# Order of the first products and of the first norm's loads in a hybrid encoder kernel

## The chip, the cores and the metric

One NeuronCore of one Trainium2 chip runs the whole program. The metric is the device time of one execution in microseconds (us). TensorE (PE) does the matrix products, VectorE (DVE) and ScalarE (ACT) the elementwise work, SyncE (SP) issues nearly all transfers; ACT issues two of them before the change.

## The reference, cut to what matters

Two layers of a trunk over 256 tokens of 1,024 values. The change touches only the first norm and the query columns of the first layer's projection:

```
h = layer_norm(x, ln_in_g, ln_in_b)
for i in range(2):
    z = h @ w_in[i]                     # columns: q 1024 | k 256 | v 256 | xr 1024 | yr | ga | gr
    attn = local_attention(rope(q), rope(k), v)
    rnn  = bidirectional_rg_lru(xr) * gelu(yr)
    h = layer_norm(a*h + (sig(ga)*(attn@w_pa) + sig(gr)*(rnn@w_pr)) @ w_out)
    h = layer_norm(a*h + ffn(h) + ple(h, p[i]))
```

Everything is float32. The kernel gets that precision from float32r products: each operand is cut into a high part (a rounded copy) and a low part (what the rounding left), and three products are summed: high x high, high x low, low x high.

## The kernel before

Tokens stand in two tiles of 128 (t = 0, 1); `c` numbers the two halves of 512 features. Weights come as items of 1 MB (128 x 2048 values). The first items are q0 part 0 (item 0), q0 part 1 (item 1), q1 part 0 (item 2), q1 part 1 (item 3), xr0 half 0 (item 4), xr0 half 1 (item 5), xr1 half 0 (item 6), the first gate block (item 7). A part of a query unit holds 512 columns for one half of the 1,024 input rows. An item is loaded into `raw`; ACT casts it to the high part (`split_hi`, L822), and DVE subtracts to get the low part (`split_lo`, L1128), which is written over `raw`. Items 0 to 3 take homes 0 to 3, item 4 takes home 4 and item 5 home 0 again, so the load of item 5 waits until TensorE is done with item 0 (`load_item`, L440: it waits for the count `s_products` that the last product on the former item gives, here `("q0", "half")`); item 6 waits in the same way for item 1, and so on.

The activations take this way: DVE takes statistics and normalises tile t (`add_ffn`, `norm_rest`: L1145 to L1175, the last four instructions are L1171 and L1174 for c = 0 and for c = 1), TensorE turns each half with four transposes into a bank (`turn_h`, L662, L654), ACT writes the high part x_hi (`x_parts`, L832), DVE the low part x_lo (`x_parts`, L1190).

Each engine runs its own list in order, written out by hand. In the first layer before the change:

- SP: rows of tile 0 (x0), item 0, the norm's gain and offset rows copied to all partitions (`load_norm`, one transfer of 1 MB), items 1 and 2, small parameters, items 3 and 4, then the waiting loads of items 5, 6 and so on.
- ACT: waits for x0, issues the rows of tile 1 (x1) and the rope table, casts item 0, x_hi of tile 0, casts items 1 and 2, x_hi of tile 1, casts items 3 and 4, empties the banks of q0, casts item 5, takes one exponential (L1019), casts item 6.
- DVE: norm of tile 0, low part of item 0, x_lo of tile 0, low part of item 1, norm of tile 1, x_lo of tile 1, low parts of items 2 to 4, `params` (L1200; it stops at L1211 for ACT's exponential), low parts of items 5, 6.
- TensorE (`token_part`, L525, twelve products of 512 columns each, four k-steps of three): q0 part 0 and part 1 for tile 0; turns of tile 1; then the other six parts, so 24 products, the turns, 72 products. Each waits until both parts of its item are there (`weights`, L519, waits for `s_split`). Behind them come the xr units with products of 256 columns.

Of the kernel before, what the change touches and what calls it, by code (L numbers as in the profile page):

```python
# [34 lines left out]
P = 128  # L35
DEPTH, SEQ, D = 2, 256, 1024
# [7 lines left out]
TT = SEQ // P  # L44
# [109 lines left out]
def in_pe_order(l):  # L154

    steps = [("q0", 0), ("q0", "half"), ("q0", 1), ("q1", "half"), ("q1", 0), ("q1", 1), ("xr0", 0), ("xr0", 1)]
    for i, name in enumerate(WITH_BLOCK):
        feature = UNITS[name][0] == "feature"
        steps += [(name, 0 if feature else "half")]
        steps += [(f"rg{i // RNN_BLOCKS}", (i % RNN_BLOCKS, g)) for g in range(2)]  # L160
        steps += [(name, 1)] if feature else [(name, 0), (name, 1)]
    steps += [(name, part) for name in ("pa0", "pa1", "pr0", "pr1") for part in ("half", 0, 1)]
    steps += [("wo0", 0), ("wo1", 0), ("wo0", "half"), ("wo1", "half"), ("wo0", 1), ("wo1", 1), ("pg0", 0)]
    steps += [("ple", (part, t)) for part in range(2) for t in range(TT)]
    steps += [("pg0", "half"), ("pg0", 1), ("pg1", "half"), ("pg1", 0), ("pg1", 1)]
    for j in range(FF_GROUPS):
        steps += [(f"{u}{j}", hh) for u in "gv" for hh in range(2)]
        if 0 < j < LAST:
            steps += [(f"d{j - 1}", part) for part in ("half", 0, 1)]
    return steps + [(f"d{LAST}", (0, 0)), (f"d{LAST}", (0, 1)), (f"d{LAST - 1}", "half"), (f"d{LAST - 1}", 1),  # L170
                    (f"d{LAST}", (1, 0)), (f"d{LAST}", "half"), (f"d{LAST}", (1, 1))]
# [31 lines left out]
RING = {}  # L203
# [44 lines left out]
def hybrid_encoder(nc, a, out):  # L248
    with ExitStack() as ctx:
# [131 lines left out]
        s_lnp = sem("lnp_loaded")  # L381
        s_small = sem("rnn_params_loaded")
# [41 lines left out]
        def _(sp):  # L424
# [38 lines left out]

            sp.dma_start(h[:, 0, :], a["x"][0, 0:P, :]).then_inc(s_h[0], 16)
            for l in range(DEPTH):
                head = ITEM[l, "q0", 0]
                load_item(head)
                load_norm(l, 0)
# [43 lines left out]
        def _(pe):  # L512
# [139 lines left out]

            def turn(dst, src):
                return nc.tensor.transpose(dst, src, ident[:])  # L654
# [64 lines left out]
            for l in range(DEPTH):  # L719
# [3 lines left out]
                if l == 0:  # L723
                    turn_h(l, 0, 0)
                x_ready(l, 1)
                token_part(l, "q0", 0, 0, x)
                x_ready(l, 2)
                token_part(l, "q0", 1, 0, x).then_inc(s_products, 1)
                turn_h(l, 0, 1, [0])
                if l:  # L730
                    token_part(l, "q1", 0, 0, x)
                turn_h(l, 0, 1, [1])
                x_ready(l, 3)
                token_part(l, "q0", 0, 1, x).then_inc(s_products, 1)
                x_ready(l, 4)
                token_part(l, "q0", 1, 1, x).then_inc(s_products, 1)
                if l == 0:
                    token_part(l, "q1", 0, 0, x)
                token_part(l, "q1", 0, 1, x).then_inc(s_products, 1)
                for t in range(TT):  # L740
                    token_part(l, "q1", 1, t, x).then_inc(s_products, 1)
# [75 lines left out]
        def _(act):  # L817
# [186 lines left out]
            act.wait_ge(s_h[0], 16)  # L1004
            act.dma_start(h[:, 1, :], a["x"][0, P:SEQ, :]).then_inc(s_h[1], 16)
            act.dma_start(rope[:], a["rope"]).then_inc(s_rope, 16)
            for l in range(DEPTH):
# [5 lines left out]
                x_parts(l, 2, [(1, 0), (1, 1)], 1.0)  # L1013
# [109 lines left out]
        def _(dve):  # L1123
# [23 lines left out]
            def norm_rest(l, n, t):  # L1147
# [20 lines left out]
                dve.wait_ge(s_lnp, 32 * l + 16 * n + 16)  # L1168
                for c in range(2):
                    at = slice(512 * c, 512 * c + 512)  # L1170
# [246 lines left out]
            for l in range(DEPTH):  # L1417
# [3 lines left out]
                if l == 0:  # L1421
                    split_to(l, "q0", 0, 0)
                    x_parts(l, 0, [(0, 0), (0, 1)], 1.0)
                    split_to(l, "q0", 1, 0)
# [175 lines left out]
```

## Time and profile before

| | us |
|---|---|
| median of 3 runs | 975.0 |
| lowest and highest run | 973.78 and 975.1 |
| the profiled execution | 974.05 |
| its span, first to last instruction | 972.2 |
| TensorE busy in it | 938.5 (97%) |
| VectorE busy | 727.5 (75%) |
| ScalarE busy | 576.1 (59%) |

1.85 us of the profiled execution lie around its span. Times in the trace count from the start of the span. Matmuls overlap, so their listed durations are longer than the distance between their starts; the sums below use the distance. In the first 16 us TensorE has only eight transposes to do; from there it is nearly always busy.

### The profile page before, as it was taken

The page shows a single profiled execution, that of the slowest core. Times are in us where ns is not written, and L with a number is a line of the kernel's source. Part 1 is how long each engine was busy: PE and PEld are TensorE (multiplying, and loading weights), DVE is VectorE, ACT ScalarE, POOL GpSimd, SP SyncE. Part 2 cuts the span into 40 slices and gives each one's busy share as a digit, 9 for nine tenths or more (in the row PEclk, how much of TensorE's full clock was granted, in tenths as well). Part 3 has the DMA queues.
Part 4 walks back from the last instruction along what each step waited for, and adds up shares of the span by engine and source line. Part 5 has one row for each costly group of instructions (what it writes and reads, how often), then busy time and mean ns, then how long its engine had stood idle before and what let it go on. Part 6 is the DMA issues. An engine that isn't in the chain of part 4 may idle for free.

```text
span 972.2 us, 12457 instructions
## 1 busy us (share of the span) xinstructions
PE 938.5 (97%) x5056; PEld 805.3 (83%) x5056; DVE 727.5 (75%) x974; ACT 576.1 (59%) x726; POOL 1.4 (0%) x9
## 2 busy tenths in 40 slices
PE   4999999999999999999999989999999999999996
PEld 3898888987788888888889879888877888888885
DVE  6778788796857876867867698888867686866755
ACT  3479789954256655546345889887434655645540
POOL 0000000000000000000000000000000000000000
PEclk9999999999999999999999999999999999999998
DMA  8455435675466556555454645455645955655621
GB/s 307 152 174 195 132 109 161 204 260 207 154 197 217 193 174 200 189 176 200 166 176 119 206 127 179 130 174 200 243 134 173 296 177 182 203 177 186 204 87 43
DMA packets 117752, 174.61 MB, mean 180 GB/s; under 512 B 3904, under 2 KB 78400, under 8 KB 117056
## 3 DMA queue, kind: packets, MB, share of 16 engines
q1 hardware_dynamic: 117408, 173.27, 53.7%
q8 instruction: 40, 0.66, 0.3%
q10 hardware_dynamic: 288, 0.56, 0.2%
q14 instruction: 16, 0.13, 0.0%
HBM read 172.76 MB, written 1.05 MB: 179 GB/s over the span
## 4 chain that ended last, share of the span: by engine, by line
PE 91%; DVE 4%; DMA 2%; ACT 2%; issue 1%; SPq 0%; DVEq 0%
PE ring L564 19%; PE ring L515 15%; PE ring L517 15%; PE ring L516 15%; PE ring L566 9%; PE misc L515 4%; PE misc L516 4%; PE misc L517 4%; PE misc L654 2%; PE misc L692 1%; PE misc L712 1%; DMA sb_r_raw<-in_w_ple_gate_dram 1%; DMA sb_lnp<-in_ln_dram 1%; DVE sb_w_lo L1128 1%; DVE sb_tmp L1294 0%
## 5 line engine op out<-in xcount | busy, mean ns | idle before, releaser
L1128 DVE TENSOR_TENSOR sb_w_lo<-sb_raw,sb_w_hi 128x2048 fp32r<-128x2048 f32 (+1 forms) x140 | 299.2, 2151 | 65.1 <-ACT sb_w_hi L822 64.9
L822 ACT CAST sb_w_hi<-sb_raw 128x2048 fp32r<-128x2048 f32 (+1 forms) x140 | 249.9, 1798 | 19.4 <-DMA sb_raw<-in_w_in_dram 4.8
L564 PE MATMUL ring<-sb_x_both,sb_w_hi 128*128 128x512 f32 x544 | 193.1, 399 | 0.0
L566 PE MATMUL ring<-sb_x_both,sb_w_lo 128*128 128x256 f32 x544 | 152.8, 281 | 0.0
L515 PE MATMUL ring<-sb_w_hi,sb_x_both 128*128 128x512 f32 x304 | 122.7, 404 | 6.4 <-DVE sb_x_both L1194 6.4
L564 PEld LDWEIGHTS ring<-sb_x_both,sb_w_hi 128*128 128x128 f32 x544 | 102.2, 188 | 25.4
L516 PE MATMUL ring<-sb_w_lo,sb_x_both 128*128 128x512 f32 x304 | 120.1, 395 | 0.0
L517 PE MATMUL ring<-sb_w_hi,sb_x_both 128*128 128x512 f32 x304 | 120.0, 395 | 0.0
L566 PEld LDWEIGHTS ring<-sb_x_both,sb_w_lo 128*128 128x128 f32 x544 | 102.8, 189 | 0.3
L515 PEld LDWEIGHTS ring<-sb_w_hi,sb_x_both 128*128 128x128 f32 x304 | 58.2, 191 | 19.3 <-DVE sb_x_both L1194 7.9
L515 PE MATMUL ring<-sb_x_both,sb_w_hi 128*128 128x256 f32 x256 | 73.0, 285 | 0.0
L517 PE MATMUL ring<-sb_x_both,sb_w_lo 128*128 128x256 f32 x256 | 72.4, 283 | 0.0
L516 PE MATMUL ring<-sb_x_both,sb_w_hi 128*128 128x256 f32 x256 | 72.4, 283 | 0.0
L517 PEld LDWEIGHTS ring<-sb_w_hi,sb_x_both 128*128 128x128 f32 x304 | 58.1, 191 | 12.7
L516 PEld LDWEIGHTS ring<-sb_w_lo,sb_x_both 128*128 128x128 f32 x304 | 58.2, 192 | 11.4
L940 ACT COPY sb_soft<-ring 128x512 f32<-128x512 f32 x24 | 14.1, 588 | 87.4 <-PE ring L566 87.4
L515 PE MATMUL misc<-sb_w_hi,sb_a_hi 128*128 128x512 f32 x144 | 56.3, 391 | 0.0
L516 PE MATMUL misc<-sb_w_lo,sb_a_hi 128*128 128x512 f32 x144 | 56.1, 390 | 0.0
L517 PE MATMUL misc<-sb_w_hi,sb_a_lo 128*128 128x512 f32 x144 | 56.0, 389 | 0.0
L836 ACT ACTIVATE sb_x_both<-misc 128x512 fp32r<-128x512 f32 x24 | 13.9, 596 | 67.8 <-PE misc L654 67.8
L516 PEld LDWEIGHTS ring<-sb_x_both,sb_w_hi 128*128 128x128 f32 x256 | 49.1, 192 | 0.1
L515 PEld LDWEIGHTS ring<-sb_x_both,sb_w_hi 128*128 128x128 f32 x256 | 49.1, 192 | 0.1
(184 smaller groups left out, 1854.7 us busy)
## 6 DMA issues: line engine op xcount, KB each, us to landing
sb_raw<-in_w_in_dram SPq DMA_DIRECT2D x42, 1024.0 KB, 5.3
sb_raw<-in_w_up_dram SPq DMA_DIRECT2D x34, 1024.0 KB, 5.3
sb_raw<-in_w_down_dram SPq DMA_DIRECT2D x18, 1024.0 KB, 4.9
sb_raw<-in_w_proj_attn_dram SPq DMA_DIRECT2D x8, 1024.0 KB, 5.1
sb_raw<-in_w_proj_rnn_dram SPq DMA_DIRECT2D x8, 1024.0 KB, 5.1
sb_hb<-in_w_up_dram SPq DMA_DIRECT2D x8, 1024.0 KB, 5.2
sb_raw<-in_w_out_dram SPq DMA_DIRECT2D x6, 1024.0 KB, 5.6
sb_raw<-in_w_ple_gate_dram SPq DMA_DIRECT2D x6, 1024.0 KB, 5.5
```

The source lines that it names most:

```text
L515: nc.tensor.matmul(dst, lhs[0], rhs[0], start=first, stop=False)
L516: nc.tensor.matmul(dst, lhs[0], rhs[1], start=False, stop=False)
L517: return nc.tensor.matmul(dst, lhs[1], rhs[0], start=False, stop=last)
L564: nc.tensor.matmul(bank_of(*key), hi[:, cols], x_both[:, k], start=k == 0, stop=False)
L566: last = nc.tensor.matmul(bank_of(*key)[:, 0:SEQ], lo[:, cols], x_hi[:, k], start=False, stop=k == KT - 1)
L654: return nc.tensor.transpose(dst, src, ident[:])
L692: last = nc.tensor.matmul(misc[:, i // 2, SEQ * (i % 2):SEQ * (i % 2 + 1)], qkT[:, GROUP * g + i, b * P:(b + 1) * P], qkT[:, HEADS + g, :] ...
L712: last = nc.tensor.matmul(misc[:, 2, :], v[:, kb, r // TT, :], pT[:, kb, :, :], start=kb == 0, stop=kb == TT - 1)
L822: nc.scalar.copy(hi_at[home][:, 0:size], raw_at[home][:, 0:size]).then_inc(s_hi_part, 1)
L836: nc.scalar.activation(x_hi[:, 4 * c:4 * c + 4, t * P:(t + 1) * P], misc[:, 2 * t + c, :].rearrange("p (k t) -> p k t", k=4), ACT.Copy, sc ...
L940: nc.scalar.copy(half_of(name)[:, hh], ring[:, pair:pair + 2, SEQ:2 * SEQ]).then_inc(s_taken, 1)
L1128: nc.vector.tensor_tensor(lo_at[home][:, 0:size], raw_at[home][:, 0:size], hi_at[home][:, 0:size].bitcast(F32), ALU.subtract).then_inc(s_s ...
```

## The change

- SP now issues: x0; the left half (columns 0 to 511 of gain and offset, 0.5 MB) of the norm's rows with a semaphore of its own; item 0; the right half (0.5 MB); x1 (moved here from ACT); items 1 and 2; the rest as before.
- DVE waits for the left half only ahead of c = 0 of tile 0, for the right half ahead of all else. It no longer takes the low parts of items 0 and 1 between the norms; it goes from x_lo of tile 0 to the norm of tile 1, and takes items 0 to 4 after x_lo of tile 1.
- ACT waits for x1 instead of x0 ahead of the rope table's issue. Item 3 is cast between x_hi of (tile 1, c = 0) and x_hi of (tile 1, c = 1).
- TensorE in the first layer first does the passes with the high weight parts (`high_pass`: eight products, x_hi and x_lo with the high part): q0 part 0, q0 part 1, q1 part 0 for tile 0, turn of (1, 0), q1 part 1 for tile 0, turn of (1, 1), the four parts for tile 1; then the 32 products with the low weight parts (`low_pass`). The number of products is the same, 96. `("q0", "half")` now comes from the low pass.
- The second layer's list is the one of before, as a function.

```diff
-    steps = [("q0", 0), ("q0", "half"), ("q0", 1), ("q1", "half"), ...]
+    steps = [("q0", 0), ("q0", "half"), ("q0", 1)] if l else [("q0", "half"), ("q0", 0), ("q0", 1)]
...
+            def load_first_norm(c, signal):
+                at = slice(512 * c, 512 * c + 512)
+                sp.dma_start(lnp[:, :, at], a["ln"][0:1, :, at].to_broadcast((P, 2, 512))).then_inc(signal, 16)
...
             sp.dma_start(h[:, 0, :], a["x"][0, 0:P, :]).then_inc(s_h[0], 16)
+            load_first_norm(0, s_lnp_left)
             for l in range(DEPTH):
                 head = ITEM[l, "q0", 0]
                 load_item(head)
-                load_norm(l, 0)
+                if l == 0:
+                    load_first_norm(1, s_lnp)
+                    sp.dma_start(h[:, 1, :], a["x"][0, P:SEQ, :]).then_inc(s_h[1], 16)
+                else:
+                    load_norm(l, 0)
...
+            def high_pass(l, name, hh, t, ready):
+                n = ITEM[l, name, hh]
+                hi = hi_at[HOME[n]]
+                pe.wait_ge(s_hi_part, n + 1)
+                if hh == 0:
+                    pe.wait_ge(s_emptied[RING[l, name, t][0]], free(l, name, t))
+                pe.wait_ge(s_x_hi, value("x_hi", l, ready))
+                for i, x in enumerate((x_hi, x_lo)):
+                    if i:
+                        x_ready(l, ready)
+                    for k in range(4):
+                        nc.tensor.matmul(bank_of(l, name, t), x[:, 4 * hh + k, t * P:(t + 1) * P],
+                                         hi[:, 512 * k:512 * k + 512], start=hh == 0 and i == 0 and k == 0, stop=False)
...
+            def first_query_units(l):
+                turn_h(l, 0, 0)
+                high_pass(l, "q0", 0, 0, 1)
+                high_pass(l, "q0", 1, 0, 2)
+                high_pass(l, "q1", 0, 0, 1)
+                turn_h(l, 0, 1, [0])
+                high_pass(l, "q1", 1, 0, 2)
+                turn_h(l, 0, 1, [1])
+                for hh in range(2):
+                    for name in ("q0", "q1"):
+                        high_pass(l, name, hh, 1, 3 + hh)
+                for name in ("q0", "q1"):
+                    low_pass(l, name, 0, 0)
+                    low_pass(l, name, 0, 1).then_inc(s_products, 1)
+                    low_pass(l, name, 1, 0).then_inc(s_products, 1)
+                    low_pass(l, name, 1, 1).then_inc(s_products, 1)
...
-            act.wait_ge(s_h[0], 16)
-            act.dma_start(h[:, 1, :], a["x"][0, P:SEQ, :]).then_inc(s_h[1], 16)
+            act.wait_ge(s_h[1], 16)
             act.dma_start(rope[:], a["rope"]).then_inc(s_rope, 16)
...
-                x_parts(l, 2, [(1, 0), (1, 1)], 1.0)
+                x_parts(l, 2, [(1, 0)], 1.0)
+                if l == 0:
+                    split_to(l, "q1", 1, 0)
+                x_parts(l, 3, [(1, 1)], 1.0)
...
                 if l == 0:
-                    split_to(l, "q0", 0, 0)
                     x_parts(l, 0, [(0, 0), (0, 1)], 1.0)
-                    split_to(l, "q0", 1, 0)
                     add_ffn(l, 1, 0)
```

## Rows read from the trace of the kernel before

**Rows 1.** The page's part 4: the chain that ended last, by engine.

```profile
PE 91%; DVE 4%; DMA 2%; ACT 2%; issue 1%; SPq 0%; DVEq 0%
```

**Rows 2.** Waits of TensorE in the whole span: total us, times, longest us.

```profile
PE misc L654 <- DVE sb_h L1174: 13.7, 5, 12.0
PE ring L515 <- DVE sb_x_both L1194: 6.4, 4, 2.2
PE misc L654 <- DVE sb_qk L1245: 4.9, 2, 2.4
```

**Rows 3.** TensorE by time: start us, us, work, [idle <- who released it].

```profile
16.11 0.80 PE L515 MATMUL ring<-sb_w_hi,sb_x_both 128*128 128x512 f32 x1 [1.69 <-DVE sb_x_both L1194]
...
24.23 0.60 PE L654 MATMUL misc<-sb_ident,sb_h 128*128 128x128 f32 x4
...
26.24 0.50 PE L515 MATMUL ring<-sb_w_hi,sb_x_both 128*128 128x512 f32 x1 [0.29 <-DVE sb_x_both L1194]
26.57 0.39 PE L516 MATMUL ring<-sb_w_lo,sb_x_both 128*128 128x512 f32 x1
...
42.67 0.28 PE L515 MATMUL ring<-sb_x_both,sb_w_hi 128*128 128x256 f32 x1
```

**Rows 4.** VectorE in order of time, 7 to 42 us.

```profile
7.53 0.16 DVE L1166 SCALAR_TENSOR_TENSOR sb_mv<-sb_mv 128x1 f32<-128x1 f32 x1
10.27 0.75 DVE L1171 SCALAR_TENSOR_TENSOR sb_h<-sb_h,sb_mv,sb_lnp 128x512 f32<-128x512 f32 x1 [2.58 <-DMA sb_lnp<-in_ln_dram]
...
19.09 1.28 DVE L1145 BATCH_NORM_STATS2 sb_st<-sb_h 128x6 f32<-128x512 f32 x2
...
36.47 0.17 DVE L1213 TENSOR_SCALAR sb_lam_t<-sb_lam_t 128x16 f32<-128x16 f32 x1 [2.13 <-ACT sb_lam_t L1019]
...
39.36 4.48 DVE L1128 TENSOR_TENSOR sb_w_lo<-sb_raw,sb_w_hi 128x2048 fp32r<-128x2048 f32 x2
```

**Rows 5.** Transfers of the first 60 us: size, us from issue to landing.

```profile
sb_lnp<-in_ln_dram SPq DMA_DIRECT2D x1, 1024.0 KB, 8.6
sb_h<-in_x_dram SPq DMA_DIRECT2D x1, 512.0 KB, 3.7
sb_h<-in_x_dram ACTq DMA_DIRECT2D x1, 512.0 KB, 6.8
```

**Rows 6.** Stretch from 4 to 10 us: the last number is GB/s moved.

```profile
4.00:10.00 6.00, 0.00 (x0) 0.00 (x0) 2.97 (x13) 3.18 (x2) 0.00 (x0) 1.00 1.03 417
```

**Rows 7.** ScalarE in order of time, 5 to 37 us.

```profile
5.32 1.28 ACT L822 ACT_TABLE_LOAD   x1 [5.32 <-DMA sb_h<-in_x_dram]
7.13 1.90 ACT L822 CAST sb_w_hi<-sb_raw 128x2048 fp32r<-128x2048 f32 x1 [0.52 <-DMA sb_raw<-in_w_in_dram]
...
14.96 3.69 ACT L822 CAST sb_w_hi<-sb_raw 128x2048 fp32r<-128x2048 f32 x2
24.86 0.60 ACT L836 ACTIVATE sb_x_both<-misc 128x512 fp32r<-128x512 f32 x1 [6.21 <-PE misc L654]
...
34.42 1.91 ACT L822 CAST sb_w_hi<-sb_raw 128x2048 fp32r<-128x2048 f32 x1 [1.83 <-DMA sb_raw<-in_w_in_dram]
```

**Rows 8.** SP's queue, 20 to 37 us: the issues of items 5 and 6.

```profile
29.26 3.09 SPq L454 DMA_DIRECT2D sb_raw<-in_w_in_dram  x2
```

**Rows 9.** The same sixteen transposes in layer 1 and layer 2.

```profile
93.28 3.57 PE L654 MATMUL misc<-sb_ident,sb_qk 128*128 128x128 f32 x16 [2.42 <-DVE sb_qk L1245]
...
565.39 1.97 PE L654 MATMUL misc<-sb_ident,sb_qk 128*128 128x128 f32 x16 [2.43 <-DVE sb_qk L1245]
```

**Rows 10.** Stretches around three stalls; granted clock is third from the end.

```profile
93.30:96.70 3.40, 3.40 (x17) 3.40 (x18) 3.40 (x3) 3.37 (x8) 0.00 (x0) 0.51 0.74 239
...
240.00:250.00 10.00, 7.82 (x35) 6.13 (x34) 7.50 (x7) 5.55 (x5) 0.00 (x0) 1.00 0.33 122
710.00:720.00 10.00, 7.76 (x28) 5.89 (x27) 6.68 (x6) 5.62 (x5) 0.00 (x0) 0.83 0.40 147
```

**Rows 11.** Waits of ScalarE from 42 to 75 us.

```profile
ACT sb_xT L843 <- PE ring L517: 8.8, 4, 4.2
```

More of the change, by code:

```diff
@@ L154, in in_pe_order @@
 def in_pe_order(l):
-    steps = [("q0", 0), ("q0", "half"), ("q0", 1), ("q1", "half"), ("q1", 0), ("q1", 1), ("xr0", 0), ("xr0", 1)]
+    steps = [("q0", 0), ("q0", "half"), ("q0", 1)] if l else [("q0", "half"), ("q0", 0), ("q0", 1)]
+    steps += [("q1", "half"), ("q1", 0), ("q1", 1), ("xr0", 0), ("xr0", 1)]
     for i, name in enumerate(WITH_BLOCK):
@@ L381, in hybrid_encoder @@
         s_lnp = sem("lnp_loaded")
+        s_lnp_left = sem("first_lnp_left_loaded")
         s_small = sem("rnn_params_loaded")
@@ new lines, in low_pass @@
+            def low_pass(l, name, hh, t):
+                hi, lo = weights(l, name, hh)
+                for k in range(4):
+                    last = nc.tensor.matmul(bank_of(l, name, t), x_hi[:, 4 * hh + k, t * P:(t + 1) * P],
+                                            lo[:, 512 * k:512 * k + 512], start=False, stop=hh == 1 and k == 3)
+                return last
+            def first_query_units(l):
[14 more added lines that the diff above has]
+                    low_pass(l, name, 1, 1).then_inc(s_products, 1)
@@ new lines, in query_units @@
+            def query_units(l):
+                x = (x_hi, x_lo)
+                x_ready(l, 1)
+                token_part(l, "q0", 0, 0, x)
+                x_ready(l, 2)
+                token_part(l, "q0", 1, 0, x).then_inc(s_products, 1)
+                turn_h(l, 0, 1, [0])
+                token_part(l, "q1", 0, 0, x)
+                turn_h(l, 0, 1, [1])
+                x_ready(l, 3)
+                token_part(l, "q0", 0, 1, x).then_inc(s_products, 1)
+                x_ready(l, 4)
+                token_part(l, "q0", 1, 1, x).then_inc(s_products, 1)
+                token_part(l, "q1", 0, 1, x).then_inc(s_products, 1)
+                for t in range(TT):
+                    token_part(l, "q1", 1, t, x).then_inc(s_products, 1)
@@ L723, in _ @@
                 if l == 0:
[L724 to L741, printed above, removed]
+                    first_query_units(l)
+                else:
+                    query_units(l)
                 feature_unit(l, "xr0")
@@ L1167, in norm_rest @@
                                                    op1=ALU.mult).then_inc(s_ln_step, 1)
-                dve.wait_ge(s_lnp, 32 * l + 16 * n + 16)
                 for c in range(2):
+                    if (l, n, t, c) == (0, 0, 0, 0):
+                        dve.wait_ge(s_lnp_left, 16)
+                    else:
+                        dve.wait_ge(s_lnp, 32 * l + 16 * n + 16)
                     at = slice(512 * c, 512 * c + 512)
```

## The prediction

> **What bounds the kernel now.** I read the chain that ended last first: TensorE holds 91% of it [rows 1], so the time can move only by when TensorE starts, by how long it is idle, and by its clock. Its list of waits has three entries [rows 2]: 12.0 us before the first transposes, four stalls for x_lo and two for the rotated queries, the longest of each 2.2 and 2.4 us. The products start at 16.11 us and the query units end at 42.67 us, where the first product of 256 columns starts [rows 3]. The change touches only what lies before. From there to the rotated queries TensorE has no wait [rows 2], so I ask when the query units end afterwards and whether an item is late behind them.
>
> What sets the start at 16.11? VectorE has its small norm steps done at 7.69 us (7.53 + 0.16) and then waits 2.58 us for the gain rows until 10.27 [rows 4]. ScalarE has the high part of item 0 long done (7.13 + 1.90 = 9.03 [rows 7]). So the left half, loaded early, attacks a real wait, and the high-first order a second one: a low part costs VectorE 2.2 us (4.48 for two [rows 4]), and one sits ahead of x_lo, which released the first product [rows 3].
>
> **Landing times after.** From 4 to 10 us the core takes in 417 GB/s [rows 6]. x0 landed at 4.43 (issued at 0.74, 3.7 us [rows 5]). I take what stands behind it on SP's queue to land in order at that rate. Test on before: item 0 would land at 4.43 + 1.05/0.417 = 6.95; ScalarE's wait for it ended at 7.13 [rows 7]. After: left half (0.52 MB) 5.7, item 0 8.2, right half 9.5, x1 10.7, and 10.8 with the slightly lower rate at the end. x1 now stands behind 2.1 MB; bounds for it are 10.0 and 11.2, the latter where it landed from ScalarE's own queue (4.43 + 6.8 [rows 5]).
>
> **The new wait on ScalarE.** It used to wait for x0; now for x1, and its queue runs in order: behind the wait stand the rope issue, the table load, the cast of item 0, x_hi. Before, the table load began 0.89 us after x0 (5.32 against 4.43 [rows 7]). So: 10.8 + 0.89 = 11.7, load 1.28, cast from 13.0, the next instruction 1.8 us later (two casts back to back take 3.69 [rows 7]), x_hi of (0, 0) from 14.8 to 15.4 (0.60 [rows 7]), first product at **15.45**. The tile's other steps are ready sooner: c = 0 is normalised at 7.7 + 1.5 = 9.2, c = 1 at 9.5 + 1.5 = 11.0, transposed by 12.2. Of the roughly 4 us that the two edits free, ScalarE's wait takes all but 0.66 us (16.11 - 15.45).
>
> **The first 24 products.** From 16.11 to the transposes at 24.23 they take 8.12 us [rows 3], which fits twelve at 0.43 and twelve at 0.23 us, so half of them run at half speed. Afterwards they are 24 as well, with an idle gap ahead of them again; I take 8.12 and keep 1 us either way for when the clock rises. Their high parts are there: items 1 and 2 are cast by 17.7 and 19.5 (15.9 + 3.69), wanted near 18.9 and 21.7; VectorE's norm of tile 1 starts at 16.7 where it started at 19.09 [rows 4], so h is early. The transposes of (1, 0) start at 15.45 + 8.12 = 23.57.
>
> **The cast of item 3.** TensorE's next pass, q1 part 1, waits for item 3's high part, and ScalarE casts it only behind x_hi of (1, 0), which waits for just these transposes. Before, x_hi began 0.63 us after the transposes did (24.86 against 24.23 [rows 3, 7]) and the next product started at 26.24, 2.01 us after them, the second turn included. After: 0.63, then the cast 0.49 behind x_hi, 1.90 long: 3.02 us, of which TensorE is idle 2.5. So 23.57 + 3.02 = 26.6; eight products 1.9 (0.33 for the first, then 0.227 each: 71 of them fill 26.57 to 42.67 [rows 3]); the second turn 0.45, now on its own (four transposes are listed at 0.60 us, which is the upper bound, with the next work overlapping them [rows 3]; the lower is half of that, 0.45 the middle); 64 products 14.5. The query units end at **43.47**, against 42.67: **+0.8 us**. In the low passes no low part is late: VectorE starts them at 30.5 and needs 2.2 each, wanted from 36.2, 38.0, 39.8 and 41.7. The extra SP issues lie under transfers that take 1.3 us and more; the rope table, now later, is wanted past 90 us.
>
> **The load of item 5.** It waits for the last product on item 0. It used to be issued at 29.26 [rows 8]; now item 0 is in use until its low pass: 28.95 + 40 x 0.227 = 38.0, issued at 38.2. It took 5.16 us to land (34.42 [rows 7]), with ample time left. After: landed 43.4, cast, the exponential at 43.4 + 1.8 = 45.2 right behind it; VectorE stands in `params` for that and resumes 0.24 us later (36.47 against 34.42 + 1.81 [rows 4, 7]): 45.4. From there to its next low part 2.89 us (36.47 to 39.36 [rows 4]): 48.3, plus 2.28 is **50.6**. TensorE wants item 5 when xr0's first half is done: 43.47 + 5.76 (48 products, 0.12 apart) = 49.2. A new stall of **1.4 us**.
>
> **Behind it.** Item 6 and the later ones have a unit of 5.8 us each to arrive. ScalarE is some 1.6 us later against TensorE when it empties the first xr bank, but it waited 8.8 us for such banks from 42 to 75 us [rows 11], so I take the lag as regained and the shift as handed on one for one.
>
> **The clock.** A stall of about 2.4 us can bring it down. The same sixteen transposes took 3.57 us behind a stall of 2.42 and 1.97 behind one of 2.43 [rows 9]; the granted clock behind the first was 0.51 (1.2 GHz) for 3.4 us [rows 10]. Of two stalls for x_lo, one left it at 1.00 (2.4 GHz), the other at 0.83 over ten us [rows 10]. Two in four, 1.6 us a time: bounds 0 and 1.6 for the new stall; I take the middle, **+0.8**, since rows of equal length lie at both ends. The Trainium skill (TensorE: Matmul & The Clock Gate, HAM oscillation) warns only of longer idle gaps; by that the term would be 0 and the time 0.8 less. The 0.51 row speaks against it.
>
> **Sum.** -0.66 (start) + 1.01 (3.02 instead of 2.01) + 0.45 (second turn) + 1.4 (item 5) + 0.8 (clock) = +3.0 us. The profiled execution took 974.05, so 977.05 by it; it lies 0.95 under the median of 975.0, which is what is compared. Forecast: 975.0 + 3.0 = **978.0**.
>
> **Rivals.**
> - *Item 5 is not late.* If its transfer or `params` is 1.4 us quicker than taken, 0.8 for the query units and 0.8 for the clock remain: 976.6; with the clock up 975.8. For it: the stall is a difference of two long sums. Against it: all its terms are rows.
> - *The lag adds up.* If ScalarE's 1.6 us isn't regained before the rotated queries, where VectorE already releases TensorE [rows 2], it comes on top: 979.6. Against it the 8.8 us of slack [rows 11].
> - *ScalarE isn't held* (the other side). If the table load and the first cast run as soon as item 0 lands at 8.2, or x1 lands far sooner, the first product waits only for the turn of c = 1 and starts at 12.1, 3.35 us sooner: 978.0 - 3.35 = 974.65, not slower; with the clock up or item 5 in time as well, under 973.05. It decides by when the cast of item 0 starts: each us before 13.0 is one of the end. Against it: before, nothing of ScalarE's list went ahead of x0 [rows 7]. The Trainium skill (ScalarE: Activation LUTs, Step-by-step: what each stage is for) has the table load placed right before the activation that needs it; by that it can't slip ahead, and the trace agrees with its 5.32.
> - *The change doesn't do what it says.* If the first pass waited for low parts after all, it would start past 18 us and end past 980. The diff shows no such wait.
>
> **How the numbers follow.** A measurement of this kernel can tell about 0.2% (1.95 us): faster is under 973.05, slower over 976.95. Forecast 0.52 (977.2 to 978.8 without and with the fall of the clock, nine in ten of it over the bound); item 5 in time 0.20 (nearly all within 0.2%); lag adds up 0.10 (slower); not held 0.14 (0.09 within, 0.05 faster); the last one 0.04 (slower). Slower 0.47 + 0.10 + 0.04 = 0.61, within 0.05 + 0.20 + 0.09 = 0.34, faster 0.05. The range takes the forecast, the first two rivals, the bounds of x1's landing (0.8 below, 0.4 above) and some of the 1 us of the clock's rise: 975.3 to 980.3. Outside lie most of "not held" and the last rival.
>
> **What would show it.** In the changed kernel: VectorE's first L1171 at about 7.7 us with no wait, ScalarE's table load near 11.7 (at 5 to 9 the forecast falls), first product near 15.45; a wait of TensorE of about 2.5 us for ScalarE's `sb_w_hi` near 24 to 26.6; first 256-column product near 43.5; a wait of about 1.4 us for VectorE's `sb_w_lo` near 49.2; the wait for rotated queries still 2.4 us. If the first product is at 12 and the two waits are small, the change gains and I am wrong in the start.

## The result, and the profile of the changed kernel

| | before | changed |
|---|---|---|
| median of 9 runs each, us | 974.0 (973.2 to 977.4) | 980.0 (977.1 to 981.3) |
| profiled execution, us | 974.05, span 972.2 | 980.0, span 978.2 |
| first product starts, us | 16.11 | 16.37 |
| first product of 256 columns (end of the query units), us | 42.67 | 45.96 |
| transposes of the rotated queries, us | 93.28 | 98.70 |

The ratio is 1.005, 95% interval 1.0037 to 1.0062: the change makes the kernel 4.9 us slower (3.6 to 6.0). The ratio is over all runs; the two medians alone are 6.0 apart. The forecast was +3.0 us. The sign is right and the 980.0 lies inside the range; the size was taken too small by about 2 us.

Runs of one kernel lie in steps of 1.5 to 2 us, and the mean granted clock goes down with each step (before: 0.996 at 971.9 us, 0.994 near 973.7, 0.992 near 975.2, 0.991 near 977.3). One fall of the clock costs about as much, 1.6 us (measured below), so a single profile can be off its kernel's median by one fall or more.

The waits of TensorE come first. A line is engine and line that wait, for whom, us in total, how often, the longest:

```profile
PE misc L725 <- DVE sb_h L1235: 12.4, 4, 9.4
PE misc L725 <- DVE sb_qk L1306: 4.9, 2, 2.4
PE ring L677 <- ACT sb_x_both L892: 2.8, 1, 2.8
PE ring L677 <- ACT sb_w_hi L878: 2.5, 1, 2.5
PE ring L527 <- DVE sb_w_lo L1186: 1.9, 1, 1.9
```

The three entries of before [rows 2] have become six; the one left out here is the wait for x_lo behind line 527, 4.6 us in two, which stood there before as well. Two entries are the forecast's: 2.5 us for ScalarE's `sb_w_hi` (item 3) and 1.9 us for VectorE's `sb_w_lo` (item 5). The 2.8 us for ScalarE's x_hi are the hold of ScalarE. What the changed kernel no longer has are the 1.69 us for x_lo ahead of the first product and the 0.29 us at tile 1 [rows 3].

TensorE's timeline up to item 5 (start, us, engine, line, what, count, idle time ahead and its releaser):

```profile
16.37 8.13 PE L677 MATMUL ring<-sb_w_hi,sb_x_both 128*128 128x512 f32 x24 [2.81 <-ACT sb_x_both L892]
24.34 0.60 PE L725 MATMUL misc<-sb_ident,sb_h 128*128 128x128 f32 x4
27.41 3.03 PE L677 MATMUL ring<-sb_w_hi,sb_x_both 128*128 128x512 f32 x8 [2.47 <-ACT sb_w_hi L878]
38.70 7.42 PE L684 MATMUL ring<-sb_w_lo,sb_x_both 128*128 128x512 f32 x32
45.96 0.28 PE L527 MATMUL ring<-sb_x_both,sb_w_hi 128*128 128x256 f32 x1
53.74 0.39 PE L527 MATMUL ring<-sb_x_both,sb_w_hi 128*128 128x256 f32 x1 [1.87 <-DVE sb_w_lo L1186]
```

The first product starts at 16.37, hardly moved. The transposes of (1, 0) start at 24.34, the next product only at 27.41. Eight products then take 3.03 us: the clock has fallen. At 53.74 the stall for item 5 ends.

What held the start, VectorE above and ScalarE below:

```profile
7.71 0.75 DVE L1232 SCALAR_TENSOR_TENSOR sb_h<-sb_h,sb_mv,sb_lnp 128x512 f32<-128x512 f32 x1
10.85 0.75 DVE L1232 SCALAR_TENSOR_TENSOR sb_h<-sb_h,sb_mv,sb_lnp 128x512 f32<-128x512 f32 x1 [1.60 <-DMA sb_lnp<-in_ln_dram]
12.12 0.38 ACTq L1061 DMA_DIRECT2D sb_rope<-in_rope_dram  x1
12.53 1.28 ACT L878 ACT_TABLE_LOAD   x1 [12.53 <-DMA sb_h<-in_x_dram]
13.83 1.90 ACT L878 CAST sb_w_hi<-sb_raw 128x2048 fp32r<-128x2048 f32 x1
```

VectorE normalises c = 0 at 7.71 with no wait, 2.56 us sooner than before [rows 4]: the left half does what it says. ScalarE takes none of that up. It waits for x1, issues the rope table at 12.12, loads its table, and casts item 0 only from 13.83, when tile 0 is already normalised (11.63 + 0.75 = 12.38) and transposed (12.44 + 1.12 = 13.56). The Trainium skill (TensorE: Matmul & The Clock Gate, Architectural detail: the array is 16× 32×32, not 1× 128×128) has ScalarE's and VectorE's queues as strictly first in, first out; the trace agrees, with everything of ScalarE's behind the wait.

Granted clock and transfer rate by stretch (busy time and instructions of each engine, then the clock as a share of full speed, the DMA engines' share, GB/s):

```profile
core 0: us, PE busy (x) PEld busy (x) DVE busy (x) ACT busy (x) POOL busy (x), PEclk, DMA share, GB/s
4.00:6.00 2.00, 0.00 (x0) 0.00 (x0) 1.41 (x4) 0.00 (x0) 0.00 (x0) 1.00 0.71 259
6.00:8.00 2.00, 0.00 (x0) 0.00 (x0) 1.76 (x11) 0.00 (x0) 0.00 (x0) 1.00 1.01 380
9.00:11.00 2.00, 1.09 (x4) 0.72 (x4) 0.40 (x2) 0.00 (x0) 0.00 (x0) 1.00 1.05 415
4.00:10.00 6.00, 0.60 (x3) 0.64 (x4) 4.38 (x15) 0.00 (x0) 0.00 (x0) 1.00 0.93 351
28.80:32.20 3.40, 3.40 (x12) 2.72 (x12) 0.24 (x1) 0.87 (x2) 0.00 (x0) 0.57 0.00 0
```

The core takes in 351 GB/s from 4 to 10 us where it took 417 [rows 6], and most of the shortfall lies in the first two us. The clock of 0.57 over the 3.4 us from 28.8 is half speed (1.2 GHz) for most of them.

The load of item 5, from SP's issue over ScalarE's cast and exponential to VectorE's low parts:

```profile
40.71 2.18 SPq L456 DMA_DIRECT2D sb_raw<-in_w_in_dram  x2
46.46 1.91 ACT L878 CAST sb_w_hi<-sb_raw 128x2048 fp32r<-128x2048 f32 x1 [3.33 <-DMA sb_raw<-in_w_in_dram]
48.51 0.17 DVE L1274 TENSOR_SCALAR sb_lam_t<-sb_lam_t 128x16 f32<-128x16 f32 x1 [4.43 <-ACT sb_lam_t L1077]
51.40 5.62 DVE L1186 TENSOR_TENSOR sb_w_lo<-sb_raw,sb_w_hi 128x2048 fp32r<-128x2048 f32 x3
```

It is issued at 40.71 where it was 29.26 [rows 8]; the cast waits for it until 46.46, the exponential until 48.27, VectorE waits 4.43 us for that and takes the low part only from 51.40, 2.34 us before TensorE gets it.

Far behind, the rotated queries' transposes and two stretches with a lower clock:

```profile
98.70 1.63 PE L725 MATMUL misc<-sb_ident,sb_qk 128*128 128x128 f32 x12 [2.42 <-DVE sb_qk L1306]
100.00:110.00 10.00, 10.00 (x44) 8.45 (x42) 8.46 (x13) 7.45 (x13) 0.00 (x0) 0.83 0.21 59
250.00:260.00 10.00, 10.00 (x39) 8.05 (x38) 8.00 (x17) 1.18 (x2) 0.00 (x0) 0.83 0.00 0
```

TensorE waits 2.42 us for the rotated queries, as before [rows 9]; they start 5.42 us later than at 93.28. So the shift of the first 54 us is handed on one for one. The span grew by 6.0. From 93 us on each profile has two falls of the clock with TensorE at work, at different places (before near 93 and at 710 to 720 [rows 10], the changed one at 100 and at 250); where the remaining 0.6 us comes from isn't shown.

The sum by these rows, against the forecast's terms:

| term | forecast | traces |
|---|---|---|
| start of the products | -0.66 | 16.37 - 16.11 = +0.26 |
| first 24 products | 0 | (24.34 - 16.37) - 8.12 = -0.15 |
| item 3's cast | +1.01 | 27.41 - 24.34 - 2.01 = +1.06 |
| second turn and the clock | +0.45 + 0.8 | (45.96 - 27.41) - (42.67 - 26.24) = +2.12 |
| item 5 | +1.4 | +1.87 |
| sum | +3.0 | +5.2 |

The fourth row can be parted by the run called filled below, in which the clock didn't fall: the second turn is +0.51 (16.94 - 16.43), the clock +1.61 (18.55 - 16.94).

### The profile page after: what moved, and what is told of

The parts are those of the page before. It is cut to its first block, busy times and chain, and to the rows that moved or that the text cites. A ratio compares the mean times of both kernels' runs of the same rounds, so it can differ in the third digit from the quotient of the medians.

```text
span 978.2 us, 12460 instructions
## 1 busy us (share of the span) xinstructions
PE 940.1 (96%) x5056; PEld 806.2 (82%) x5056; DVE 727.0 (74%) x974; ACT 575.7 (59%) x726; POOL 1.4 (0%) x9
## 4 chain that ended last, share of the span: by engine, by line
PE 89%; DVE 4%; DMA 3%; ACT 2%; issue 1%; SPq 0%; ACTq 0%; DVEq 0%
PE ring L576 18%; PE ring L527 14%; PE ring L528 14%; PE ring L529 14%; PE ring L578 9%; PE misc L527 4%; PE misc L529 4%; PE misc L528 4%; PE misc L725 2%; PE ring L677 2%; PE misc L763 1%; PE misc L783 1%; DMA sb_r_raw<-in_w_ple_gate_dram 1%; ACT sb_w_hi L878 1%; DMA sb_h<-in_x_dram 1%
## 5 line engine op out<-in xcount | busy, mean ns | idle before, releaser
L527 PE MATMUL ring<-sb_w_hi,sb_x_both 128*128 128x512 f32 x272 | 109.5, 403 | 4.6 <-DVE sb_x_both L1255 4.6
L528 PE MATMUL ring<-sb_w_lo,sb_x_both 128*128 128x512 f32 x272 | 107.2, 394 | 0.0
L529 PE MATMUL ring<-sb_w_hi,sb_x_both 128*128 128x512 f32 x272 | 107.0, 393 | 0.0
L527 PEld LDWEIGHTS ring<-sb_w_hi,sb_x_both 128*128 128x128 f32 x272 | 51.9, 191 | 15.7 <-DVE sb_x_both L1255 5.4
L529 PEld LDWEIGHTS ring<-sb_w_hi,sb_x_both 128*128 128x128 f32 x272 | 51.8, 190 | 11.3
L528 PEld LDWEIGHTS ring<-sb_w_lo,sb_x_both 128*128 128x128 f32 x272 | 51.8, 191 | 10.1
```

The source lines that it names most:

```text
L527: nc.tensor.matmul(dst, lhs[0], rhs[0], start=first, stop=False)
L528: nc.tensor.matmul(dst, lhs[0], rhs[1], start=False, stop=False)
L529: return nc.tensor.matmul(dst, lhs[1], rhs[0], start=False, stop=last)
```

## The experiments

Each was measured beside the kernel before on the same chip, 11 or 12 runs each, halves_swapped 6; before's own median was 973.9 to 975.0. The differences (95% interval) are the ratio to before, less one, times 974. "256" is the start of the first product of 256 columns, "qk" that of the rotated queries' transposes, both from the profile.

| kernel | median, us | against before, us | 256 | qk |
|---|---|---|---|---|
| before | | | 42.67 | 93.28 |
| changed | 980.0 | +4.9 (3.6 to 6.0) | 45.96 | 98.70 |
| order_only | 975.0 | +0.3 (-1.2 to 1.8) | 42.77 | 94.91 |
| loads_only | 976.5 | +2.0 (0.2 to 3.8) | 45.37 | 95.99 |
| act_free | 976.3 | +1.8 (0.6 to 2.9) | 41.56 | 93.61 |
| cast3_early | 975.2 | -0.5 (-1.8 to 0.9) | 40.76 | 92.78 |
| exp_early | 977.0 | +2.8 (1.4 to 4.4) | 45.73 | 96.34 |
| filled | 977.4 | +2.0 (0.3 to 3.9) | 44.00 | 96.64 |
| left_behind | 979.9 | +4.4 (2.8 to 5.8) | 45.18 | 97.39 |
| halves_swapped | 978.5 | +4.9 (3.1 to 6.7) | 45.34 | 97.54 |
| all_three | 971.3 | -3.0 (-4.8 to -1.3) | 39.94 | 90.55 |
| order_mended | 972.4 | -2.0 (-3.3 to -0.8) | 40.01 | 90.62 |
| item3_sooner | 972.4 | -2.4 (-3.7 to -1.2) | 39.35 | 89.97 |
| loads_free | 973.8 | +0.9 (-0.6 to 2.2) | 43.9 | 94.49 |

The columns 256 and qk are the sharper measure of a place, but they hold luck too: TensorE's first 24 products, the same work in all kernels, take 6.9 to 8.4 us from profile to profile. They start 0.43 us apart and end 0.23 apart, and what differs is when the one becomes the other (the clock column reads 1.00 throughout, so that this shows in the distances alone).

**The order alone** (the changed kernel with before's loads, x1 on ScalarE's queue):

```diff
             sp.dma_start(h[:, 0, :], a["x"][0, 0:P, :]).then_inc(s_h[0], 16)
-            load_first_norm(0, s_lnp_left)
...
-                if l == 0:
-                    load_first_norm(1, s_lnp)
-                    sp.dma_start(h[:, 1, :], a["x"][0, P:SEQ, :]).then_inc(s_h[1], 16)
-                else:
-                    load_norm(l, 0)
+                load_norm(l, 0)
...
-            act.wait_ge(s_h[1], 16)
+            act.wait_ge(s_h[0], 16)
+            act.dma_start(h[:, 1, :], a["x"][0, P:SEQ, :]).then_inc(s_h[1], 16)
...
```

> The changed kernel with the loads of before: one transfer for the norm's rows behind item 0, tile 1's rows from ScalarE's queue, ScalarE waiting for tile 0's rows only. Theory: first product behind the second turn near 14.5 (x_hi was at 13.07 before), the stall at item 3's cast of 2.5 us and that before xr0's second half of 1.2 to 1.9 us stay; 0.5 to 1.5 us slower than before, plus the clock's fall in some runs. Rival (the high-first order by itself gains): faster than before by 1 us or more.

```profile
13.90 7.48 PE L672 MATMUL ring<-sb_w_hi,sb_x_both 128*128 128x512 f32 x24
24.29 3.68 PE L672 MATMUL ring<-sb_w_hi,sb_x_both 128*128 128x512 f32 x8 [2.47 <-ACT sb_w_hi L873]
49.96 0.39 PE L522 MATMUL ring<-sb_x_both,sb_w_hi 128*128 128x256 f32 x1 [1.28 <-DVE sb_w_lo L1182]
```

The products start 2.2 us sooner than before, since none of them waits for a low part. All of it is given back: item 3's stall of 2.47 us with the clock's fall behind it (eight products in 3.68 us) brings the end of the query units to 42.77, where it was, and item 5 costs 1.28. The high-first order by itself is worth nothing here, as its casts and loads stand.

**The loads alone** (before, with the halves, x1 on SP and ScalarE's wait for it; order of products, casts and low parts as before), its wait alone:

```diff
...
-            act.wait_ge(s_h[0], 16)
-            act.dma_start(h[:, 1, :], a["x"][0, P:SEQ, :]).then_inc(s_h[1], 16)
+            act.wait_ge(s_h[1], 16)
...
```

> The kernel before with the load edits alone: halves of the first norm's rows, tile 1's rows on SP's queue, ScalarE waiting for them; the products in the old order. Theory: ScalarE is held to 12.1, cast of item 0 to 15.7, then its low part and x_lo on VectorE: first product near 18.6 instead of 16.1, no stalls at item 3 and item 5; 2.5 us slower than before, about 976.5. Rival (the loads help and the order of the products costs everything): first product at 14 or sooner and faster than before.

```profile
12.38 1.28 ACT L833 ACT_TABLE_LOAD   x1 [12.38 <-DMA sb_h<-in_x_dram]
18.55 0.80 PE L526 MATMUL ring<-sb_w_hi,sb_x_both 128*128 128x512 f32 x1 [5.17 <-DVE sb_x_both L1207]
```

The table load begins at 12.38 where it was 5.32 [rows 7], and the first product 2.44 us later than before. The halves are there, yet the loads as a whole cost 2.0 us by the ratio and 2.7 at both places of the profile.

**ScalarE not held** (the changed kernel, with ScalarE waiting for x0 ahead of the rope table; nothing else):

```diff
-            act.wait_ge(s_h[1], 16)
+            act.wait_ge(s_h[0], 16)
             act.dma_start(rope[:], a["rope"]).then_inc(s_rope, 16)
```

> The changed kernel with one edit: ScalarE waits for the rows of tile 0, not of tile 1, ahead of the rope table's issue. Theory (ScalarE is held by tile 1's rows): table load near 5.4, cast of item 0 near 9 to 11, first product right behind the second turn near 13.6 instead of 16.37, the other waits as they are; 2.8 us less than the changed kernel, about 976 to 977. Rival (the start is bound by the transfers or by VectorE, and the wait is hidden): first product stays near 16, time within 0.5 us of the changed kernel.

```profile
5.24 1.28 ACT L878 ACT_TABLE_LOAD   x1 [5.24 <-DMA sb_h<-in_x_dram]
9.44 1.90 ACT L878 CAST sb_w_hi<-sb_raw 128x2048 fp32r<-128x2048 f32 x1 [2.91 <-DMA sb_raw<-in_w_in_dram]
13.27 5.70 PE L677 MATMUL ring<-sb_w_hi,sb_x_both 128*128 128x512 f32 x16
24.62 2.13 PE L677 MATMUL ring<-sb_w_hi,sb_x_both 128*128 128x512 f32 x8 [2.47 <-ACT sb_w_hi L878]
```

One constant moves the first product from 16.37 to 13.27, 3.10 us. That is the price of the hold, and the ratios say the same (+1.8 instead of +4.9). Item 3's stall stays at 2.47 us, here without a fall of the clock. Behind the earlier start a wait of 0.63 us for item 2's cast is new, and the wait for item 5's low part is 1.2 us.

**Item 3's cast ahead of x_hi of (1, 0):**

```diff
-                x_parts(l, 2, [(1, 0)], 1.0)
                 if l == 0:
                     split_to(l, "q1", 1, 0)
+                x_parts(l, 2, [(1, 0)], 1.0)
                 x_parts(l, 3, [(1, 1)], 1.0)
```

> The changed kernel with one edit: ScalarE casts item 3 ahead of x_hi of (1, 0), not behind it. Theory (the cast order makes TensorE's stall at 25 to 27 us and with it the fall of the clock): that stall of 2.47 us is gone or under 0.5, the clock stays up there, the slower group of runs gets rarer; 2.5 us less without the clock, up to 4 us with it, about 976 to 977. Rival (item 3's transfer or VectorE's norm of tile 1 is next): a stall of over 1.5 us stays at the same place with another releaser.

```profile
16.25 7.40 PE L677 MATMUL ring<-sb_w_hi,sb_x_both 128*128 128x512 f32 x24 [2.81 <-ACT sb_x_both L892]
23.49 0.60 PE L725 MATMUL misc<-sb_ident,sb_h 128*128 128x128 f32 x4
23.84 2.10 PE L677 MATMUL ring<-sb_w_hi,sb_x_both 128*128 128x512 f32 x8
```

The stall is gone: product follows transposes after 0.35 us. No other wait comes in its place. At qk this kernel is 5.92 us ahead of the changed one, and the rows give each piece: start 0.12, first 24 products 0.73 (7.24 instead of 7.97; the clock rose sooner), transposes to product 2.72 (0.35 instead of 3.07), from there to the products of 256 columns 1.63 (16.92 instead of 18.55), item 5 0.71. Item 3's wait and the fall behind it are the largest single cost: 5.4 us by the ratios, 4.35 us (2.72 + 1.63) by the rows that belong to them. Without them the kernel can't be told from before.

**The exponential ahead of item 5's cast:**

```diff
-                split_to(l, "q1", 0)
-
+                if l:
+                    split_to(l, "q1", 0)
                 act.wait_ge(s_param_step, value("param_step", l, 1))
                 nc.scalar.activation(lam_t[:, 1], lam_t[:, 0], ACT.Exp).then_inc(s_param_exp, 1)
+                if l == 0:
+                    split_to(l, "q1", 0)
```

> The changed kernel with one edit: ScalarE takes the exponential that VectorE's parameter steps wait for ahead of the cast of item 5. Theory (item 5 is late because its cast, the exponential, the parameter steps and its low part stand in one chain): the stall of 1.87 us before xr0's second half is gone, VectorE takes the low part at once behind the cast, 1.9 us less than the changed kernel. Rival (the landing of item 5 alone makes it late): the stall stays over 1 us.

```profile
43.61 0.22 ACT L1077 ACTIVATE sb_lam_t<-sb_lam_t 128x16 f32<-128x16 f32 x1 [0.71 <-DVE sb_lam_t L1268]
45.68 1.90 ACT L878 CAST sb_w_hi<-sb_raw 128x2048 fp32r<-128x2048 f32 x1 [1.85 <-DMA sb_raw<-in_w_in_dram]
47.62 2.29 DVE L1188 TENSOR_TENSOR sb_w_lo<-sb_raw,sb_w_hi 128x2048 fp32r<-128x2048 f32 x1 [0.77 <-ACT sb_w_hi L878]
```

VectorE does its parameter steps while item 5 is still under way and waits only 0.77 us for the cast. TensorE has no wait for a low part any more; qk is 2.36 us sooner than in the changed kernel, of which 0.23 was there at 256 already; the ratios say 2.1. So the late load is not the cost by itself: the cost is that `params` stood between its cast and its low part.

**The stall of item 3 filled** with twenty transposes of the identity, whose result nobody reads (extra work; the result of the kernel is as before):

```diff
                 turn_h(l, 0, 1, [0])
+                for _ in range(20):
+                    turn(misc[:, 3, 0:P], ident[:])
                 high_pass(l, "q1", 1, 0, 2)
```

> The changed kernel with 20 transposes of the identity into an unused place, put where TensorE stands idle for item 3's cast; the computation is otherwise whole. Theory (the idle stretch brings the clock down in some runs): the stall's length stays (products resume near 27.4), the granted clock stays 1.00 from 27 to 32 us in the profile, and the upper group of runs (980 and over) vanishes, median near 977.5. Rival (the clock falls by something else, such as the phase of the earlier start): the clock falls behind it all the same and the upper group stays at about half of the runs.

```profile
27.06 2.12 PE L677 MATMUL ring<-sb_w_hi,sb_x_both 128*128 128x512 f32 x8 [0.30 <-ACT sb_w_hi L880]
27.00:32.00 5.00, 4.94 (x24) 4.08 (x25) 1.71 (x2) 2.35 (x3) 0.00 (x0) 1.00 0.00 0
```

TensorE waits as long as it did (the next product starts at 27.06, 0.35 sooner than in the changed kernel, since its first 24 products took less), but is idle for only 0.30 us of it. The clock stays at 1.00, eight products take 2.12 us, and from 27.06 to 44.00 pass 16.94 us instead of 18.55: **1.61 us is the price of the fall.** The ratios say 2.9, but their intervals (3.6 to 6.0 and 0.3 to 3.9) allow 1.6 as well. Of the six profiles with this stall unfilled (changed, order_only, exp_early, left_behind, halves_swapped, act_free), five show the fall; since one doesn't, filled's profile alone would be weak evidence, and its runs have to speak as well. The upper group didn't vanish but nearly did, as expected: one of 12 runs is at 980 us or over, where the changed kernel has five of 9, and the median of its runs' mean clocks is 0.994 instead of 0.992.

**Which half is slow.** Two kernels ask why x1 landed late: the left half behind item 0, and the two halves swapped (the right one first).

```diff
-            load_first_norm(0, s_lnp_left)
...
                 if l == 0:
+                    load_first_norm(0, s_lnp_left)
                     load_first_norm(1, s_lnp)
```

> The changed kernel with the left half of the norm's rows issued behind item 0, ahead of the right half. In the changed kernel the rate fell to 215 GB/s from 4 to 5 us, and tile 1's rows landed 1.3 us later than worked out. Theory (the small strided transfer right behind the first one leaves the engines short): from 4 to 7 us the rate is over 380 again, tile 1's rows land near 11.0, and with them table load, cast and first product come 0.9 us sooner, near 15.5; about 1 us less than the changed kernel. Rival (the halves cost the same wherever they stand): the landing stays near 12 and the first product near 16.3.

```profile
4.00:6.00 2.00, 0.00 (x0) 0.00 (x0) 1.72 (x7) 0.00 (x0) 0.00 (x0) 1.00 1.05 399
6.00:8.00 2.00, 0.00 (x0) 0.00 (x0) 1.25 (x7) 0.00 (x0) 0.00 (x0) 1.00 0.94 257
```

```diff
-            load_first_norm(0, s_lnp_left)
+            load_first_norm(1, s_lnp_left)
...
-                    load_first_norm(1, s_lnp)
+                    load_first_norm(0, s_lnp)
...
-                    if (l, n, t, c) == (0, 0, 0, 0):
+                    if (l, n, t, c) == (0, 0, 0, 1):
```

> The changed kernel with the right half of the norm's rows loaded at the first place and the left one behind item 0; VectorE needs the left one first, so its c = 0 waits for it. Theory (a half is slow by its place as the first transfer of these rows, not by which columns it holds): the rate from 4 to 6 us is again under 320 GB/s, and tile 1's rows land near 12 as in the changed kernel; the first product stays near 16.3 since ScalarE sets it. Rival (the left columns themselves are slow): the rate falls behind item 0, from 7 to 9 us, instead.

```profile
4.00:6.00 2.00, 0.00 (x0) 0.00 (x0) 1.29 (x2) 0.00 (x0) 0.00 (x0) 1.00 0.90 250
```

The slow stretch moves with the first half (257 GB/s from 6 to 8 us when it goes behind item 0) and does not care which columns it holds (250 from 4 to 6 us with the right one first). The second half runs at the common rate (415 GB/s from 9 to 11 us in the changed kernel, while it lands). Neither kernel differs from the changed one in time by more than the intervals: with ScalarE held, x_hi waits for ScalarE, and it is of no use that VectorE is early. I had put left_behind's rate over 380 until 7 us and its first product at 15.5; the slow stretch only moved, x1 was late all the same (ScalarE released at 11.77), and the product came at 16.01.

**All three edits together** (ScalarE free, item 3's cast and the exponential early):

> The changed kernel with the three edits together: ScalarE waits for tile 0's rows only, casts item 3 ahead of x_hi of (1, 0), takes the exponential ahead of the cast of item 5. Theory (the three waits are what eats the gain, and they add up): first product near 13.3, none of the three stalls over 0.7 us, first 256-column product near 39.5 instead of 42.67, about 3 us less than the kernel before: 971.5. Rival (the transfers are next: items 1 to 3 land too late for the earlier products): a stall of 1 us or more for a high part whose cast waited for its transfer, and less than 2 us of gain.

```profile
21.06 1.90 ACT L878 CAST sb_w_hi<-sb_raw 128x2048 fp32r<-128x2048 f32 x1 [1.58 <-DMA sb_raw<-in_w_in_dram]
13.24 8.41 PE L677 MATMUL ring<-sb_w_hi,sb_x_both 128*128 128x512 f32 x24
23.02 2.11 PE L677 MATMUL ring<-sb_w_hi,sb_x_both 128*128 128x512 f32 x8 [0.93 <-ACT sb_w_hi L878]
```

This beats both kernels: -3.0 us against before. One wait is left, 0.93 us at 23.02, where I had expected none over 0.7. It is for item 3's transfer, as the rival had it: the cast itself waited 1.58 us for its data until 21.06.

**The same without the load edits** (order_only with item 3's cast and the exponential moved):

> The changed kernel with the loads of before and the two edits of ScalarE's order (cast of item 3 ahead of x_hi of (1, 0), exponential ahead of the cast of item 5): the high-first order with its stalls taken out and no halves. Theory (the order of the products is worth about 2 us once ScalarE keeps up; the halves add at most 1 us more): first product near 14.2, no stall over 0.7 us, about 2 to 3 us less than before, within 1 us of all_three. Rival (the halves carry the gain of all_three): no faster than before.

```profile
14.02 7.06 PE L672 MATMUL ring<-sb_w_hi,sb_x_both 128*128 128x512 f32 x24
23.06 2.12 PE L672 MATMUL ring<-sb_w_hi,sb_x_both 128*128 128x512 f32 x8 [1.55 <-ACT sb_w_hi L873]
```

I expected no wait above 0.7 us; there is one of 1.55, and again it is item 3's transfer (the cast waited 2.51 us, until 21.11). This start is 0.78 us later than in all_three, and at the end of the query units 0.07 is left of it (40.01 against 39.94), since both wait for item 3's landing. The 0.78 was gone before that, mostly by luck with the clock: the first 24 products took 8.25 us in all_three (13.24 to 21.49) and 6.89 here (14.02 to 20.91). -2.0 us with the order and the two moves alone is clear of zero, so the gain doesn't need the loads. What the loads add, 1.0 us by the ratios, lies within the intervals (-4.8 to -1.3 and -3.3 to -0.8): it isn't shown that they help with ScalarE free, nor that they don't.

**Item 3 loaded sooner** (all_three, item 3 ahead of the small parameters on SP's queue):

```diff
-                for n in range(head + 1, head + 3):
+                ahead = 3 if l else 4
+                for n in range(head + 1, head + ahead):
                     load_item(n)
```

> all_three with item 3 loaded ahead of the small parameters. In all_three ScalarE waited for item 3's transfer until 21.06 and TensorE idled 0.93 us for its cast. Theory (the small transfers hold SP's queue up): the cast starts about 1 us sooner and that idle time is under 0.2 us, up to 0.9 us less than all_three. Rival (the bytes ahead of it set the landing): the cast starts within 0.3 us of 21.06 and the time stays.

```profile
4.59 3.52 SPq L456 DMA_DIRECT2D sb_raw<-in_w_in_dram  x1
19.61 2.14 PE L678 MATMUL ring<-sb_w_hi,sb_x_both 128*128 128x512 f32 x8 [0.60 <-ACT sb_w_hi L879]
22.42 2.12 PE L678 MATMUL ring<-sb_w_hi,sb_x_both 128*128 128x512 f32 x8 [0.23 <-ACT sb_w_hi L879]
```

Item 3's cast begins 0.6 us sooner (20.46), its wait is 0.23, and one of 0.60 for item 2's high part is new, so the waits fall only from 0.93 to 0.83; the query units end 0.59 sooner. The ratios can't tell it from all_three. Neither side is borne out: the cast moved by more than the rival's 0.3 and less than the theory's 1 us, and the theory's reason is wrong. Small transfers don't hold SP's queue by being small: item 3 in their place holds it as long (3.52 us from 4.59, against 3.26 from 4.75 for the small parameters in all_three). The eighth transfer of the list waits until about 8.1 us, whichever it is; what it waits for isn't shown. The same step without the halves was not run.

**The loads with ScalarE free, in the old order** (loads_only with ScalarE's wait on x0):

> The kernel before with the halves and tile 1's rows on SP's queue, but ScalarE waiting for tile 0's rows only; products in the old order. Theory: the norm of tile 0 ends at 12.4 instead of 13.26, then item 0's low part and x_lo as before, first product near 15.3 instead of 16.1: up to 0.8 us less than before, hard to tell from it. Rival (the halves are worth the 2.6 us by which VectorE's first wait ends sooner): first product near 13.5.

```profile
15.25 0.79 PE L526 MATMUL ring<-sb_w_hi,sb_x_both 128*128 128x512 f32 x1 [1.69 <-DVE sb_x_both L1207]
23.74 0.66 PE L665 MATMUL misc<-sb_ident,sb_h 128*128 128x128 f32 x4 [0.78 <-DVE sb_h L1187]
26.00:28.00 2.00, 2.00 (x6) 1.61 (x6) 1.49 (x2) 2.00 (x2) 0.00 (x0) 0.59 0.00 0
```

The first product comes at 15.25, 0.86 us sooner than before, as expected, but no gain arrives. VectorE's norm of tile 1 now ends later than the turn of it is wanted (0.78 us at 23.74, 0.79 at 25.19), and the clock fell right behind (0.59 from 26 to 28 us, where before had 1.00). +0.9 us with an interval across zero doesn't settle whether the halves help or harm in the old order.

## Why the prediction was right in sign and too small

- **What bounds, and where to look**: right. Nothing behind 54 us has a new wait, and the 5.42 us at the rotated queries against 5.2 by the sum say that the shift is handed on.
- **The left half and VectorE**: right, 7.71 with no wait.
- **ScalarE's new wait**: right as a mechanism; act_free prices it at 3.10 us. The size was off: x1 was taken to land at 10.8, outside bound 11.2, and ScalarE was released at about 12.1. The rate of 417 GB/s [rows 6] was carried over to a list of transfers with a new member, and with it the core took in 259 for two us. By my estimate from these two rates that is 0.8 of the 1.3 us (2 us x 158/417); x0 landing 0.11 later and 380 to 414 GB/s behind it fit the rest. 0.5 us of it was given back by luck: the 0.89 us from landing to table load, taken from before, held two issues on ScalarE's queue, x1's and the rope table's, and the change takes x1's away, so it was 0.41 (12.12 to 12.53). The start was +0.26 instead of -0.66, 0.9 us of the 2.2 missing.
- **The first 24 products**: 7.97 for 8.12, right, but with luck: the same 24 took 7.24 in cast3_early and 6.89 in order_mended, so the 1 us kept for the clock's rise was needed and a little short.
- **Item 3's cast**: right to 0.05 us (3.07 for 3.02; the wait 2.47 for 2.5). cast3_early confirms the cause.
- **The second turn**: 0.51 for 0.45, right.
- **The clock**: the mechanism was right, its size half, and this is the term that was sized worst together with the start: 0.8 us of the 2.2 missing. I took 0.8, the middle between "no fall" and "a fall" for want of more than four stalls. Here the fall came in five of six, at 1.61 us behind item 3's stall. Two stalls in four and five in six are few; but where the cost has two values and nothing in between, the forecast of a single time should have named one. The Trainium skill (TensorE: Matmul & The Clock Gate, HAM oscillation) warns only of longer idle gaps than this; the runs differ, with 2.47 us of idle time, 0.57 of the clock behind it in the changed kernel and 1.00 in filled.
- **Item 5**: the chain through `params` as told, 1.87 us for 1.4, 0.5 us of the 2.2 missing. The issue came at 40.71 instead of 38.2, but TensorE, on whose products it waits, was late by as much (45.96 instead of 43.47), so only the landing counts: 5.75 us after the issue instead of 5.16. exp_early confirms that the chain is the cause.
- **The lag of ScalarE**: regained, as taken; the wait for the rotated queries is 2.42 in both.
- **The rivals**: "item 5 is not late" falls by the 1.87 us, "the lag adds up" by the unchanged 2.42, "ScalarE isn't held" by the 12.53 of its table load. With one constant changed (act_free) the last one is near in its price, 3.10 us for 3.35, but not in the rest: the first product comes at 13.27, not at 12.1, since the right half lands late too, and the kernel is still 1.8 us slower than before.

The chances, which gave slower 0.61, leaned on "item 5 in time" (0.20) and "not held" (0.14). Both rested on doubt in sums whose every term was a row, and the traces bear these sums out to 0.5 us for item 5's stall and 0.8 for the table load (12.53 for 11.7), each on the side of slower.

## What to carry to other kernels

A wait put at the head of an in-order queue delays all that stands behind it: ask of each what it needs itself (the rope table needed nothing of x1, and the wait cost 3.1 us). When the order of the products changes, the other engines' lists must change with it: here the cast of item 3 and the exponential still stood where the old order wanted them, and with the two moved the same order of products went from +0.3 us (-1.2 to 1.8) to -2.0 (-3.3 to -0.8). A new idle gap of TensorE of about 2.5 us should be priced with the clock's fall behind it, 1.6 us here, as the likely case, and a shorter one isn't free of it (next section).

## What was not expected of the hardware

While the first half of the gain rows comes in (0.5 MB, each row of 2 KB written to all 128 partitions), the core's rate is down to 242 to 274 GB/s for two us, in each of the eleven profiles with halves, whether it stands ahead of item 0 or behind it and whichever columns it holds. Around the second half it isn't (415 from 9 to 11 us in the changed kernel), nor was it with the whole 1 MB in before (407 and 443 GB/s from 4 to 8 us, by the same view). A slow first touch of these rows would fit the halves but not the 1 MB of before; why is open.

The clock fell in five of six profiles behind an idle gap of 2.47 us and stayed up in one (act_free), with the same gap to 0.01 us; what tells the one from the five isn't shown. Length alone doesn't: the clock fell behind two gaps of 0.8 us close together in loads_free, and stayed up behind single gaps of 0.93 us (all_three), 1.55 (order_mended) and 1.87 (item 5 in the changed kernel).
